# Cross-attention on one Trainium2 core: the memory's values in slices, and the seventh tile's output products in three pieces

## The reference

```
q = (x @ wq).reshape(b, s, XA_HEADS, XA_DIM)
k = (mem @ wk).reshape(b, m, XA_HEADS, XA_DIM)
v = (mem @ wv).reshape(b, m, XA_HEADS, XA_DIM)
sc = einsum('bshd,bmhd->bhsm', q, k) * XA_DIM ** -0.5
p = softmax(sc)
o = einsum('bhsm,bmhd->bshd', p, v).reshape(b, s, XA_W)
x = layer_norm(alpha * x + o @ wo, g, b)
```

## Time and profile before

| | us |
|---|---|
| median of three timed runs | 1007.88 (1007.2 to 1008.26) |
| the profiled execution, its own time | 1005.39 |
| span from its first to its last instruction | 1003.6 |
| TensorE busy | 967.9 (96%) |
| VectorE busy | 590.5 (59%) |
| ScalarE busy | 350.5 (35%) |
| GpSimd busy | 191.5 (19%) |

### The profile page before, as it was taken

One profiled execution on the slowest core, in us unless ns is written; L12 is line 12 of the kernel. 1 busy time (PEld: TensorE's weight loads), 2 busy tenths in 40 slices (PEclk: granted clock), 3 DMA queues, 4 the chain that ended last, 5 costly groups with the idle time before them and its releaser, 6 DMA issues. The chain is left out here.

```text
span 1003.6 us, 15741 instructions
## 1 busy us (share of the span) xinstructions
PE 967.9 (96%) x5687; PEld 834.8 (83%) x5687; DVE 590.5 (59%) x1271; ACT 350.5 (35%) x737; POOL 191.5 (19%) x248
## 2 busy tenths in 40 slices
PE   7999999999899999999999999999899999999995
PEld 6899887787779999988876888888888989898984
DVE  7734340778566666555556364458634376767676
ACT  6122031444465454511023333332223243434342
POOL 0013100121043210002220000003400034333335
PEclk9999999999999999999999999999999999999998
DMA  9122010002799100250013200042688888989972
GB/s 315 50 80 84 1 64 1 1 1 84 295 413 355 58 23 22 86 229 1 25 59 129 85 1 1 1 163 98 262 274 295 269 304 289 311 301 322 320 276 93
DMA packets 67278, 151.60 MB, mean 151 GB/s; under 512 B 8720, under 2 KB 16144, under 8 KB 67216
## 3 DMA queue, kind: packets, MB, share of 16 engines
q1 hardware_dynamic: 59920, 133.82, 37.9%
q0 software_dynamic: 7296, 16.95, 4.4%
HBM read 107.62 MB, written 52.03 MB: 159 GB/s over the span
## 5 line engine op out<-in xcount | busy, mean ns | idle before, releaser
L1941 PEld LDWEIGHTS h_ps<-xgT,e_gate_up 128*128 128x128 f32 x1024 | 155.6, 192 | 4.5 <-issue 2.2
L1941 PE MATMUL h_ps<-xgT,e_gate_up 128*128 128x176 f32 x1024 | 157.1, 315 | 2.2 <-issue 2.2
L262 PE MATMUL unit_ps<-whi,xhi 128*128 128x512 f32 (+1 forms) x256 | 97.9, 382 | 5.9 <-DVE wlo L294 5.9
L263 PE MATMUL unit_ps<-wlo,xhi 128*128 128x512 f32 (+1 forms) x256 | 97.5, 381 | 0.0
L264 PE MATMUL unit_ps<-whi,xlo 128*128 128x512 f32 (+1 forms) x256 | 97.5, 381 | 0.0
L1001 PEld LDWEIGHTS o_ps<-mla_v,prob_T 128*128 128x128 f32 x576 | 69.9, 192 | 9.2 <-issue 6.0
L1001 PE MATMUL o_ps<-mla_v,prob_T 128*128 128x64 f32 x576 | 71.5, 274 | 3.4 <-ACT prob_T L1073 3.0
L262 PEld LDWEIGHTS unit_ps<-whi,xhi 128*128 128x128 f32 x256 | 48.4, 189 | 13.5 <-DVE xlo L338 5.8
L2084 DVE SCALAR_TENSOR_TENSOR z<-y_ps,slot_weight,x_rows 128x512 f32<-128x512 f32 (+1 forms) x64 | 45.7, 746 | 22.4 <-PE y_ps L1955 21.6
L264 PEld LDWEIGHTS unit_ps<-whi,xlo 128*128 128x128 f32 x256 | 48.3, 189 | 7.8
L263 PEld LDWEIGHTS unit_ps<-wlo,xhi 128*128 128x128 f32 x256 | 48.5, 189 | 7.6
(11 more groups left out here) (337 smaller groups left out, 2134.0 us busy)
## 6 DMA issues: line engine op xcount, KB each, us to landing
e_gate_up<-w_gu SPq DMA_DIRECT2D x16, 2048.0 KB, 10.8
e_down_raw<-w_dn SPq DMA_DIRECT2D x16, 1024.0 KB, 5.3
slot_rows<-zeros SPq DMA_DIRECT2D x22, 522.0 KB, 6.2
slot_sums<-zeros SPq DMA_DIRECT2D x22, 512.0 KB, 6.3
x_rows<-slot_rows SPq DMA_DIRECT2D x16, 522.0 KB, 4.7
slot_sums<-z SPq DMA_DIRECT2D x16, 512.0 KB, 4.5
wraw<-w_in SPq DMA_DIRECT2D x24, 256.0 KB, 4.4
xraw<-xT SPq DMA_DIRECT2D x16, 256.0 KB, 4.8
```

The costliest lines, as they stand in the source:

```text
L262: pe.matmul(o, hi, whi[:, s, 0:w], start=(s == 0), stop=False)
L263: pe.matmul(o, hi, wlo[:, s, 0:w], start=False, stop=False)
L1941: end = pe.matmul(hps[:, m, gu * CAP:(gu + 1) * CAP], gate_up[:, b, s, w], xT[:, s, :], start=(s == 0), stop=(s == KD - 1))
```

## The change

`outputs` and `memory_values` get an argument that names the slices to compute; the count at the end (`summed`, `v_sum`) is given only with the last slice. Nothing is computed that was not computed before. On TensorE the order changes at these places:

- Round 0: the first slice of `memory_values(1)` goes ahead of `turn_queries(0)`, the second behind it, ahead of `scores(0)`; the other six stay where all eight were.
- Rounds 1 and 2: `turn(t + 1)` goes from behind `scores(t)` to ahead of it.
- Rounds 7 and 8: of `outputs(6)` only the first two heads stay at the end of round 7. The third goes behind `turn_probs(7)`, ahead of `values(7)`; the fourth behind `turn_x2(5)`, ahead of `logits(5)`. `summed` for tile 6 is counted with the fourth.

The programs of the other engines are the same.

```diff
-            def outputs(t):
+            def outputs(t, parts=range(XH)):
                 pe.wait_ge(o_lo, t + 1)
...
-                for s in range(XH):
+                for s in parts:
...
-                last.then_inc(summed, 1)
+                if parts[-1] == XH - 1:
+                    last.then_inc(summed, 1)
...
-            def memory_values(m):
+            def memory_values(m, parts=range(KD)):
                 pe.wait_ge(k.wv_loaded, 16 * KD)
-                for s in range(KD):
+                for s in parts:
                     last = pe.matmul(acc[:, m, :], k.memT[:, s, m * P:(m + 1) * P], k.wv[:, s, :], start=(s == 0), stop=(s == KD - 1))
-                last.then_inc(v_sum, 1)
+                if parts[-1] == KD - 1:
+                    last.then_inc(v_sum, 1)
...
                 if t:
                     turn_probs(t - 1)
+                if t == NT:
+                    outputs(NT - 2, range(2, 3))
                 if t < NT:
                     queries(t, range(4, KD))
                 if t:
                     values(t - 1)
+                if t == 0:
+                    memory_values(1, range(0, 1))
                 if t < NT:
                     turn_queries(t)
-                if t >= 3:
+                if t == 0:
+                    memory_values(1, range(1, 2))
+                elif t < 3:
+                    turn(t + 1)
+                else:
                     turn_x2(t - 3)
+                if t == NT:
+                    outputs(NT - 2, range(3, XH))
                 if t < NT:
                     scores(t)
                 if t >= 3:
                     logits(t - 3)
-                if t + 1 < NT:
+                if t == 0 or 3 <= t < NT - 1:
                     turn(t + 1)
                 if t == 0:
-                    memory_values(1)
+                    memory_values(1, range(2, KD))
                 if t == NT:
                     place(0)
                 if t:
-                    outputs(t - 1)
+                    outputs(t - 1, range(2) if t == NT - 1 else range(XH))
```

## The result

The changed kernel is slower, by 0.36%.

The account below looks back on a forecast made before the run. Bounds: TensorE's own order mid-block, its waits for ScalarE's copies in rounds 0 to 2, VectorE from 677 us to `outputs(7)`. -2.65 + 4.1 + 0.2 = +1.65 us, put on the median, gave 1009.5 us, range 1006.9 to 1011.9.

Parts of the forecast that it names:

- The bound: From 677 us to the start of `outputs(7)` the block waits for VectorE, so TensorE's idle gaps there win nothing.
- Round 0, 1.65 us: Two TensorE gaps, 0.85 and 0.90 us, each take one 0.86 us slice of the memory's values: 1.65 us gained.
- Rounds 1 and 2, 1.0 us: Turning ahead of the scores fills 0.90 us gaps; VectorE's low part limits the gain to 0.5 us a round.
- `residual(6)` late by 4.1 us: Rounds 7 and 8: the late `summed` delays VectorE's `residual(6)` and everything queued behind it, through `place(0)`: cost 4.1 us.
- Order as a whole: The gain of rounds 0 to 2 and the cost in rounds 7 and 8 together: -2.65 + 4.1 = +1.45 us.
- The clock, +0.2 us: A low stretch on `outputs(7)` costs 1.5 us after the change against 1.3 now: 0.2 us more.
- (a): Rival: longer idleness ahead of `place(0)` puts following products at low clock, another 1.3 to 1.9 us, 1010.8 to 1011.4; chance 0.17.
- (b): Rival: work queued behind `residual(6)` on VectorE has slack, so only rounds 0 to 2 count: 1003.9 to 1005.2; chance 0.07.
- (c): Rival: rounds 0 to 2 give nothing, as products between the transposes delay them or the copies: 1012.2; chance 0.05.
- (d): Rival: the unexplained 1.9 us delay of ScalarE's last `negated` vanishes: 1008.5; chance 0.16, shared with a mild clock.
- The rule: By the skill's page alone, a clock fall would be new with the change, the sum higher by 1.3 us.
- Placing the sum on a median: The change was put on the timed runs' median, 1007.88 us, as the profiled execution lay 2.5 us below it.

Follow-up runs that it names:

- front_only: The changed kernel with `outputs(6)` in one piece again, so only the change in rounds 0 to 2; 1006.01 us, ratio 0.9972 to the kernel before.
- q_front: `front_only` plus the fillers of `q_before`, products of no use in two later idle times of TensorE; 1005.37 us, ratio 0.9983 to the kernel before.
- q_before: The kernel before plus products of no use: two at the block's end, three behind the first expert's gate products; 1010.10 us, ratio 1.0011.
- tail_only: The changed kernel with rounds 0 to 2 as before, so only the three pieces of `outputs(6)`; 1014.86 us, ratio 1.0054 to the kernel before.
- q_after: The changed kernel plus the fillers of `q_before`; 1012.21 us, ratio 1.0045 to the kernel before.
- early_choice: The changed kernel with VectorE's `rank_experts(0)` at the end of round 6 and `choose(0)` in round 7; 1008.61 us, ratio 0.9996 to the kernel before.
- rank_first: The changed kernel with VectorE's `rank_experts(0)` ahead of `residual(6)` instead of behind it; 1008.42 us, ratio 0.9986 to the kernel before.
- filled: The changed kernel with 14 products of no use on TensorE ahead of `place(0)`; 1012.83 us, ratio 1.0043 to the kernel before.
- filled_both: The changed kernel with 14 products of no use ahead of `place(0)` and 7 ahead of `logits(5)`; 1011.58 us, ratio 1.0035 to the kernel before.
- q_filled: `filled_both` plus the fillers of `q_before`; 1009.16 us, ratio 1.0022 to the kernel before.
- front_early_piece: `front_only` with VectorE's routing moved as in `early_choice` and the fourth head of `outputs(6)` behind `turn_probs(7)`; 1007.50 us, ratio 0.9995 to the kernel before.

## Why the prediction was wrong

**The bound: right.** VectorE held `place(0)` before the change, and holds it after: VectorE's cast ends at 688.19 us and `place(0)` starts at 688.24.

**Round 0, 1.65 us: right.** Measured 1.74 at tile 0's turning of the probabilities. **Rounds 1 and 2, 1.0 us: right.** The gain grows to 45.38 - 43.15 = 2.23 at tile 1 and to 2.74 at tile 2, 0.49 and 0.51 for the two rounds. The queries' start right behind the low part stands in the trace at 562.57. All profiles with the front have the same distances within 0.1 us, and in timed runs `front_only` is 2.8 us faster, `q_front` 2.9 us faster than `q_before`.

**`residual(6)` late by 4.1 us: right.** The idle gap of VectorE is 4.18 us, and 4.20 in `tail_only`, and `place(0)` comes 4.04 us later there. Order as a whole was forecast at -2.65 + 4.1 = +1.45 and is +1.24 (`q_after` against `q_before`: +1.40). That ScalarE's copy and `copy_x2(5)` wait for the fourth head was seen too, and that the filled gaps are worth nothing; the forecast did not say that this second path holds the logits back longer than before (1.66 against 1.11 us) and keeps the pieces from gaining anything even with VectorE's queue empty, as `early_choice` showed.

**The clock, +0.2 us: this step failed, by about 2 us.** That the clock falls again was right; what it costs more than before was mis-sized, with two errors. First, I took the 1.3 us that `outputs(7)` paid in the one profile of before for its usual price. It was the exception: of the five kernels with `outputs(6)` whole, four paid nothing (6.98 in before; 5.65, 5.66, 5.66, 5.68 in the others; mean 5.93 us). `q_before` has the same two gaps of 1.11 us and no fall of the clock. Second, I priced the fall after the change at 1.5 us, between the costs of the two stretches of 3.3 and 3.4 us that the profile of before has. It is one of 10.2 us (6.8 in some kernels) that begins at the logits behind the new wait of 1.66 us, runs through the 3.76 us of idleness where it costs nothing, and has 4.7 us left for `outputs(7)`. Three profiles with the pieces and the long idle time have 7.88, 8.52 and 7.77 us, mean 8.06. The term is 8.06 - 5.93 = **2.1 us** by the profiles; the timed runs give the estimate of 1.6 ± 0.9 above.

**The sum, mended.** +1.24 for order and +2.1 for the clock make +3.4 us; measured are +3.6 (2.0 to 5.1). Both terms are from profiles, and the sum's agreement is as good as the interval is wide, not better.

**The rivals.** (a), the clock decides, came nearest: products start in a low stretch and the next, at 1.9 us more than forecast where it said 1.3 to 1.9. Its cause it had half right: it blamed the idle time ahead of `place(0)`, and the fall comes before that, behind the 1.66 us ahead of the logits. It had 0.17, because one row of one profile seemed to say that the price was already paid. (b) fell: nothing in VectorE's queue had slack. (c) fell, by `front_only`; that its number, 1012.2, is the measured median is chance. (d) did come in the profile: ScalarE's last `negated` waits 3.95 us in before alone and 2.05 us in the 13 other profiles, `q_before` among them, and 1.4 us of that are on the path. It was an accident of the one execution that I read, so it is no gain of the change.

**The rule.** The Trainium skill ("TensorE: Matmul & The Clock Gate", "Why this matters for your kernels") asks for no long idle gaps between bursts of matmuls, and means longer ones than those of the earlier trace rows. I set it aside, since the clock had fallen after two gaps of 1.11 us. With more profiles one thing speaks for it: with both gaps of 1.11 us and `outputs(6)` whole, `outputs(7)` ran at full clock in four of five. By the rule the sum was to be higher by 1.3 us, which was the better number. But the falls after the change are not what it describes: they come after 1.66 us of idleness and ahead of the long idle time, and `rank_first` and `early_choice`, with no gap above 1.66 us, had low stretches of 6.8 us all the same. So the better number owed something to luck.

**Placing the sum on a median.** The median of 1007.88 us was of three runs. With 20 runs it is 1008.32, and over the three other groups 1007.98 to 1009.59: another 0.4 us of the miss.

## What to carry to other kernels

A count that stands at the end of a group of products releases every engine's queue behind it: whoever splits the group to fill one engine's gaps has to read, engine by engine, what stands behind the waiter. Here 2.2 us of gaps were filled on an engine that was waiting for VectorE, at a price of 4.0 us at `place(0)`. A gap made longer on TensorE can also be paid by the products behind it, at half clock, and it need not be the longest one: here 1.66 us in place of 1.11 ahead of small products went with the fall in six profiles of six. Price it from several profiles of the kernel before, as a low stretch seen in one may be that run's alone.

## What the runs showed of the hardware

**Low clock time goes with most of the scatter of a kernel's runs.** From each timed run's mean granted clock, 2 x (1 - clock) x span is its time at 1.2 GHz. Over the 35 runs of before in the first group it has a correlation of 0.91 with the run's time, at 0.39 us for each us (0.86 and 0.76 in the other two groups). Its mean was 23.1 us in those 35 runs, and 31.4 us in the 20 of the changed kernel (`tail_only` 31.2, `early_choice` 30.0, `filled` 28.0, `rank_first` 25.2, `filled_both` 23.4, `front_only` 21.8; `q_before` 19.7, `q_after` 27.8, `q_filled` 16.6, `q_front` 18.1). So the timed runs show, too, that the changed kernel spends 8 us more at the low clock, on average and not in one profile. The six kernels with 1.66 us of idleness ahead of the logits all have means of 25.2 us or more, and all others but `front_early_piece` (27.8) 23.9 or less. What this costs does not follow from it: 3.8 us of the changed kernel's low stretch fall on idle time, and `filled_both`, with 8 us less of low time than the changed kernel, was timed no faster.

**The clock also falls where the code is the same.** Between 260 and 280 us of the span, on code ahead of the block, the profiles have 1.2 GHz for no time (`rank_first`, `q_before`), 3.4 us (before, `front_only`), 6.8 us (after and six others, and `q_after` in two pieces) or 10.2 us (`tail_only`, `early_choice`), and the block began at 520.6 to 527.1 us. What decides it stays open.

**Fillers must come before the fall.** 14 of them took 5.69 us behind it; with seven more ahead of the logits it did not come in either of two profiles (`filled_both`, `q_filled`), and the 14 no longer delayed `place(0)` (166.05 against 165.96).
